# State-space sums in four row strips and four PSUM banks, VectorE's jobs in a new order, and the second attention's heads split as they are normed

## The chip, the cores and the metric

The kernel runs on one core of one Trainium2 chip. Its time is device time in microseconds (us). Before the change three runs took 2142.61, 2143.15 and 2150.36 us; their median, 2143.15 us, is the time before. All stages run one after another on the same core, and five engines work side by side: TensorE (PE in the profile, its weight loads PEld), VectorE (DVE), ScalarE (ACT), GpSimd (POOL) and SyncE (SP), which issues the DMAs.

## The reference, cut to what matters

The program is two layers of a hybrid block (attention, convolution, retention, MLP) and then one block of another kind, on 512 positions of width 1024, all in float32. The change lies in the last block:

```python
xn = rmsnorm(h, norm1_gain)
q, k, v, u, gates = split(xn @ w_in)
q = rope(rmsnorm(q, q_norm_gain)); k = rope(rmsnorm(k, k_norm_gain))
# 8 heads, each a difference of two softmaxes; o is 512 x 128 per head
o = diff_attention(q, k, v, lam)
attn_branch = rmsnorm(o, subln_gain) * (1 - lam_init) @ w_attn_proj
# s5: u (512 wide) -> complex states x_t = lb * x_{t-1} + B u_t, y = Re(C x) + D u
xr, xi = scan(lb, u @ B);  y = C_re @ xr - C_im @ xi + d * u
s = gelu(y) * sigmoid(gelu(y) @ w_glu + b_glu);  ssm_branch = s @ w_ssm_proj
h = h + (sigmoid(g_attn) * attn_branch + sigmoid(g_ssm) * ssm_branch) @ w_out
```

## The kernel before, in words

Nearly all of the time goes to dense products in a three-term form. Each float32 operand is split into a high and a low part (fp32r), and a product is hi*hi + lo*hi + hi*lo. A **piece** is twelve such matmuls of 128x128 weights by 512 columns (`accumulate`, L711 is its matmul). Four pieces use one weight unit of 1 MB. For each unit SP loads `raw`, ACT copies the high part (`w_hi`, L1356) and POOL subtracts to make the low part (`w_lo`, L518).

Each engine has a program of its own, written out in order. They meet only at semaphores. `fullN` says that PSUM bank N holds a result, `freeN` that it may be written again; `fill(b)` on PE waits for `freeN`. A tuple of numbers says behind which piece each side job stands: `p` counts the pieces of the last block's input products, and PE runs `hook(p)` behind piece p, while ACT and DVE walk through the same p and put their share at the same place in their own order. PE waits only where a semaphore is late.

The jobs of the stage that the change touches:

- **State sums.** For each of four blocks of 128 channels: `sums_in(blk)` on PE (L1010, behind pieces 8, 12, 16, 20) multiplies the inputs `uT` by `b_pow` into banks 4 (real) and 5 (imaginary). Each matmul has only 32 rows; the rows lie in one of four strips of the array, and two strips run at a time. After each of four rounds PE waits for `strip_done`. `states(blk, stage)` on DVE turns the sums by sine and cosine (stage 0, six instructions, L2341 to L2349), runs eight scans (stage 1, L2355) and turns back (stage 2, six instructions, L2360 to L2366). `sums_out(blk)` on PE (L1024, L1031, behind pieces 14, 18, 22, 26) waits for the states; `skip` on DVE (L2371) adds the input and frees bank 6.
- **Turn tables.** `turns(b)` on POOL (L643 to L648, six instructions) makes the sine and cosine of block b, between the `w_lo` units of this stage.
- **The kernel of the short response.** `short_response` (L995) behind piece 10.
- **Norm of q by columns.** `q_columns(n)` on PE (L1041, behind pieces 9 and 17) makes the mean squares of eight half heads, with 128 columns of `q_square` as weights and two moving columns, sixteen matmuls. DVE copies them out (`q_mean`, L2381) and so frees bank 7.
- **Rotation.** ACT moves a partner tile by four DMAs (`fetch_partner`, L1692; the third and later wait for the rotation two before), DVE rotates (`rotate`, L2398 to L2401, three instructions).
- **Norm of k.** `k_mean(j)` on PE (L1051) behind pieces 22, 24, 26, 28, 30, 36, 38 and 42; it fills bank 7, which the norm of the k before frees.

After the pieces comes the second attention: 32 steps (8 heads of 4 tiles), with 32 gate pieces laid between them by `GATE_STEPS`. PE makes scores (L822), transposes (L1116) and values (L1129). When a head is whole, ACT squares it (`o_square`, L1827), PE takes its mean (L822 too, `one(O_MEAN, ...)`), ACT and DVE take the root and norm the head. The gate pieces read `act_hi` and `act_lo`, and the normed heads are split into the same two tiles, so all eight splits stand at steps 32 to 37 (`heads_split`), behind the last gate pieces. The attention's projection starts after that.

## Time and profile before

| What | Value |
|---|---|
| median of three runs | 2143.15 us (2142.61 to 2150.36) |
| the profiled execution | 2144.72 us, its span 2142.9 us |
| PE busy | 2100.7 us, 98% of the span |
| DVE, ACT, POOL busy | 1061.5, 876.3, 925.4 us |
| pieces 9 to 30 with their jobs | 1296.7 to 1423.4 us from the span's start |
| second attention | 1511.6 to 1678.0 us |

All times are microseconds from the start of the span. A row of the timeline gives start, length, engine, line, operation, tiles and count; in square brackets the idle time before it and what ended that. Instructions of one engine overlap in the pipeline, so a matmul's own length is more than its share of time: the distance of starts tells the pace. PEclk is the clock that TensorE was granted, 1.00 being 2.4 GHz and 0.50 being 1.2 GHz.

### The profile page before, as it was taken

What the parts mean: (1) busy time and instruction counts of PE and PEld (TensorE: products, weight loads), DVE (VectorE), ACT (ScalarE), POOL (GpSimd) and SP (SyncE); (2) the same over time, 40 slices, a digit from 0 to 9 for tenths busy, and PEclk for the clock granted to TensorE, in tenths of its full rate; (3) what the DMA queues carried; (4) which work ended last, traced back from release to release, by engine and by line L of the source; (5) the groups of instructions that cost most, each with busy time, mean ns of one, the idle gap of its engine ahead of it and who ended that gap; (6) DMA issues with size and microseconds to landing.
All of it is one profiled execution on the core that took longest, in us unless ns stands there. A gap on an engine that the chain in (4) does not pass through costs nothing.

```text
span 2142.9 us, 27507 instructions
## 1 busy us (share of the span) xinstructions
PE 2100.7 (98%) x10200; PEld 1676.2 (78%) x10200; DVE 1061.5 (50%) x1725; ACT 876.3 (41%) x1219; POOL 925.4 (43%) x306
## 2 busy tenths in 40 slices
PE   8999999999999999999999999999999899999999
PEld 7875888888888776888888888877766787888887
DVE  5866242222247654422222258985588534554555
ACT  5345462223243445533222343164566534333332
POOL 5522444443455333545654456333312254444442
PEclk9999999999999999999999998899999999999999
DMA  5431213223224331233222242223111232322232
GB/s 182 150 117 71 77 63 98 97 98 98 99 69 149 125 93 46 79 99 98 94 100 87 92 148 85 66 84 108 60 60 60 95 100 81 97 88 90 97 98 78
DMA packets 120050, 202.29 MB, mean 94 GB/s; under 512 B 6544, under 2 KB 51856, under 8 KB 119696
## 3 DMA queue, kind: packets, MB, share of 16 engines
q1 hardware_dynamic: 112992, 189.12, 26.7%
q10 hardware_dynamic: 6960, 11.88, 1.9%
q8 instruction: 60, 0.98, 0.2%
q14 instruction: 38, 0.31, 0.0%
HBM read 189.44 MB, written 8.12 MB: 92 GB/s over the span
## 4 chain that ended last, share of the span: by engine, by line
PE 75%; issue 16%; POOL 3%; DVE 3%; ACT 1%; ACTq 1%; DMA 0%; POOLq 0%; DVEq 0%; SPq 0%
PE bank L711 63%; PE bank L813 5%; POOL w_lo L518 3%; PE bank L822 1%; PE bank L1010 1%; PE bank L765 1%; PE bank L840 1%; PE bank L880 1%; PE bank L774 1%; PE bank L868 0%; ACTq L1572 0%; DVE pr L2018 0%; PE bank L1041 0%; ACTq L1692 0%; PE bank L906 0%
## 5 line engine op out<-in xcount | busy, mean ns | idle before, releaser
L518 POOL TENSOR_TENSOR w_lo<-raw,w_hi 128x2048 fp32r<-128x2048 f32 (+1 forms) x167 | 741.9, 4442 | 1119.3 <-ACT w_hi L1356 1119.3
L711 PE MATMUL bank<-act_hi,w_hi 128*128 128x512 f32 x1488 | 595.6, 400 | 5.9 <-DVE hid L2561 2.5
L711 PE MATMUL bank<-act_hi,w_lo 128*128 128x512 f32 x1488 | 584.7, 393 | 0.0
L711 PE MATMUL bank<-act_lo,w_hi 128*128 128x512 f32 x1488 | 584.1, 393 | 0.0
L1356 ACT ACTIVATE w_hi<-raw 128x2048 fp32r<-128x2048 f32 (+1 forms) x170 | 314.2, 1848 | 591.2 <-PE bank L711 545.8
L711 PEld LDWEIGHTS bank<-act_hi,w_hi 128*128 128x128 f32 x1488 | 282.5, 190 | 78.0 <-issue 11.8
L711 PEld LDWEIGHTS bank<-act_hi,w_lo 128*128 128x128 f32 x1488 | 281.9, 189 | 60.7
L711 PEld LDWEIGHTS bank<-act_lo,w_hi 128*128 128x128 f32 x1488 | 282.5, 190 | 58.2 <-issue 1.4
L711 PE MATMUL bank<-h_hi,w_hi 128*128 128x512 f32 x704 | 277.7, 394 | 0.3 <-DVE x L2526 0.3
L711 PE MATMUL bank<-h_lo,w_hi 128*128 128x512 f32 x704 | 277.4, 394 | 0.0
L711 PE MATMUL bank<-h_hi,w_lo 128*128 128x512 f32 x704 | 277.4, 394 | 0.0
L2263 DVE TENSOR_TENSOR f<-f,bank 128x512 f32<-128x512 f32 x128 | 88.1, 688 | 238.7 <-PE bank L711 238.7
L2249 DVE SCALAR_TENSOR_TENSOR hid<-bank,rrow 128x512 f32<-128x512 f32 x64 | 43.7, 691 | 250.3 <-PE bank L711 245.3
L711 PEld LDWEIGHTS bank<-h_hi,w_hi 128*128 128x128 f32 x704 | 131.7, 187 | 33.4 <-DVE h_lo L2080 0.7
L711 PEld LDWEIGHTS bank<-h_hi,w_lo 128*128 128x128 f32 x704 | 131.7, 187 | 32.7
L711 PEld LDWEIGHTS bank<-h_lo,w_hi 128*128 128x128 f32 x704 | 131.7, 187 | 32.1
L2556 DVE TENSOR_TENSOR bank<-bank,rrow 128x512 f32<-128x512 f32 x44 | 30.7, 699 | 142.9 <-PE bank L711 140.4
L813 PE MATMUL bank<-act_hi,w_hi 128*128 128x512 f32 x192 | 76.3, 398 | 5.7 <-DVE act_lo L1940 5.2
L534 POOL TENSOR_TENSOR sums<-sums,squares 128x512 f32<-128x512 f32 x50 | 64.6, 1292 | 37.4 <-ACT squares L1374 35.1
L1993 DVE SCALAR_TENSOR_TENSOR bank<-ypad,lcol,bank 128x512 f32<-128x512 f32 x116 | 76.6, 755 | 0.0
L813 PE MATMUL bank<-act_hi,w_lo 128*128 128x512 f32 x192 | 74.8, 390 | 0.0
L813 PE MATMUL bank<-act_lo,w_hi 128*128 128x512 f32 x192 | 74.8, 389 | 0.0
(362 smaller groups left out, 2638.5 us busy)
## 6 DMA issues: line engine op xcount, KB each, us to landing
raw<-in_w_up SPq DMA_DIRECT2D x32, 1024.0 KB, 5.4
raw<-in_w_down SPq DMA_DIRECT2D x32, 1024.0 KB, 5.0
raw<-in_w_in SPq DMA_DIRECT2D x26, 1024.0 KB, 5.1
raw<-in_w_up SPq DMA_DIRECT2D x44, 512.0 KB, 4.6
raw<-in_w_in SPq DMA_DIRECT2D x28, 768.0 KB, 4.5
raw<-in_w_out SPq DMA_DIRECT2D x12, 1024.0 KB, 5.0
raw<-in_w_down SPq DMA_DIRECT2D x22, 512.0 KB, 4.2
raw<-in_w_attn_proj SPq DMA_DIRECT2D x4, 1024.0 KB, 5.1
```

Of the source, the lines that this page charges most:

```text
L518: pool.tensor_tensor(m.w_lo[slot][:, 0:n], m.raw[slot][:, 0:n], m.w_hi[slot][:, 0:n].bitcast(F32), ALU.subtract).then_inc(s["split_ready"], 1)
L534: ins = pool.tensor_tensor(m.sums[:], m.sums[:], m.squares[n % 4][:], ALU.add)
L711: mm = pe.matmul(o, ll if i == 2 else lh, rl if i == 1 else rh, start=first and n == 0, stop=last and n == len(steps) - 1)
L765: mm = pe.matmul(bank[b][:, t:t + 1], x[:, t * P:(t + 1) * P], m.per_d, start=(part == 0), stop=(part == 1))
L774: mm = pe.matmul(bank[b][:, t * P:(t + 1) * P], column[:, t:t + 1].to_broadcast([P, P]), m.ident, start=True, stop=True)
L813: mm = pe.matmul(bank[b][:], (wl if i == 2 else wh)[:, k % KU, cols], (m.act_lo if i == 1 else m.act_hi)[:, k, :], start=(k == 0 and i == ...
L822: pe.matmul(bank[b][:] if o is None else o, lhsT, rhs, start=True, stop=True).then_inc(s[f"full{b}"], 1)
L1356: act.activation(m.w_hi[slot][:, 0:n], m.raw[slot][:, 0:n], ACT.Copy).then_inc(s["w_hi"], 1)
L1993: ins = dve.scalar_tensor_tensor(to, y, w, sums, ALU.mult, ALU.add)
L2249: dve.scalar_tensor_tensor(m.hid[:, b, :], bank[b][:], 0.0, m.rrow[:], ALU.max, ALU.mult).then_inc(s[f"free{b}"], 1)
L2263: dve.tensor_tensor(sums, sums, bank[4 + b][:], ALU.add).then_inc(s[f"free{4 + b}"], 1)
L2556: dve.tensor_tensor(bank[b][:], bank[b][:], m.rrow[:], ALU.mult).then_inc(s["up_scaled"], 1)
```

## The change

What it does, part by part:

1. `sums_in` writes each row strip's sums to a bank of its own (4, 5, 6, 7; real part in columns 0 to 127, imaginary in 128 to 255). The four strips alternate matmul by matmul, and the waits for `strip_done` are gone. `states` reads all four banks as one tile of PSUM, and frees all four behind its fifth instruction. So `sums_in` now also needs banks 6 and 7.
2. `states` stages 0 and 1 stand one piece earlier, behind pieces 8 and 9, and so ahead of the rotations. The rotations are spread one per piece.
3. `q_columns` becomes two steps: `q_rows` (behind 10 and 18; four matmuls of 512 columns, each into 32 rows of bank 7), a copy by ACT, and four matmuls of 8 columns behind 11 and 19. In `jobs` on ACT the copy stands behind that piece's `fetch_partner`.
4. `short_response` moves from behind piece 10 to behind piece 6.
5. The turn tables get a tile per block. Block 0's is made during the layer before, blocks 1, 2 and 3 follow two units earlier than they did, behind the stage's first, second and third `w_lo`. They no longer wait for the states.
6. The normed heads are split into tiles of their own (`a_hi` over `k2`, `a_lo` over `q2`), each two steps behind its mean, so seven of the eight stand inside the attention. The mean stands a step later. Head 7's mean stands behind the first piece of the projection. The gate pieces stand in steps 0 to 27, 29, 31, 33 and 34.

The diff, cut to its core:

```diff
-        m.bank = [ctx.enter_context(nc.psum_tensor(f"bank{i}", [P, T], F32)) for i in range(8)]
+        m.bank = [ctx.enter_context(nc.psum_tensor(f"bank{i}", [P, T], F32)) for i in range(4)]
+        m.quad = ctx.enter_context(nc.psum_tensor("bank4", [P, 4, T], F32))
+        m.bank += [m.quad[:, i, :] for i in range(4)]
...
+    m.a_hi = ar("a_hi", [P, KD, T], 16, F32R)
+    m.a_lo = ar("a_lo", [P, KD, T], 0, F32R)
...
-    m.both = put("both", [P, T], at=x_at + 2048 * 5)
-    m.sin_n, m.cos_n = ([put(f"{name}{i}", [P, T], at=x_at + 2048 * (6 + k) if i == 0 else arena + 1024 * (36 + 2 * k)) for i in range(2)]
-                        for k, name in enumerate(("sin_n", "cos_n")))
+    m.both = ar("both", [P, T], 14)
+    m.sin_n, m.cos_n = ([ar(f"{name}{i}", [P, T], at + 2 * k) for i, at in enumerate((36, 28, 24))] +
+                        [put(f"{name}3", [P, T], at=x_at + 2048 * (5 + k))] for k, name in enumerate(("sin_n", "cos_n")))
...
+    def turns(b):
+
+        shape = [P, 4, TURN_A, TURN_B]
+        wide = lambda x: x[:].rearrange("p (s a b) -> p s a b", s=4, a=TURN_A)
+        sin, cos, both = wide(m.sin_n[b]), wide(m.cos_n[b]), wide(m.both)
...
+        if b == 3:
+            pool.wait_ge(s["x_parked"], 16)
...
-            for _ in range(U_MLP - 4 - 4 - 15):
+            lo()
+            for _ in turns(0):
+                lo()
+            for _ in range(U_MLP - 4 - 4 - 15 - 3):
...
-    pool.wait_ge(s["trig_ready"], 2)
+    whole(turns(1))
     lo()
-    turns(0)
+    whole(turns(2))
     lo()
-    turns(1)
-    lo()
-    turns(2)
-    lo()
-    turns(3)
-    lo()
-    lo()
+    whole(turns(3))
+    for _ in range(4):
...
-        fill(4)
-        fill(5)
+        for b in QUAD:
+            fill(b)
         if blk == 0:
             pe.wait_ge(s["u_ready"], 4)
             pe.wait_ge(s["param_dve"], N_PARAM_B)
-        for r in range(4):
+        for part in range(2):
             for j in range(SUB):
-                for part in range(2):
-                    q = (r + part) % 4
-                    mm = pe.matmul(bank[4 + part][:, q * P:(q + 1) * P], m.b_pow[strips[q], SUB - 1 - j, part, blk, :],
+                for q, b in enumerate(QUAD):
+                    mm = pe.matmul(bank[b][:, part * P:(part + 1) * P], m.b_pow[strips[q], SUB - 1 - j, part, blk, :],
                                    m.uT[strips[q], blk, j * N_SUB:(j + 1) * N_SUB], start=(j == 0), stop=(j == SUB - 1))
-                    if j == SUB - 1:
-                        mm.then_inc(s["strip_done" if r < 3 else f"full{4 + part}"], 1)
-            if r < 3:
-                pe.wait_ge(s["strip_done"], c.up("strip_done", 2))
+                    if part == 1 and j == SUB - 1:
+                        mm.then_inc(s[f"full{b}"], 1)
...
+    def q_rows(n):
 
         pe.wait_ge(s["q_squared"], c.up("q_squared", 4))
         fill(7)
         for j in range(4):
-            for t in range(NT):
-                mm = pe.matmul(bank[7][:, 0:8 * NT].rearrange("p (c j t) -> p c j t", c=2, t=NT)[:, :, j, t], m.q_square[j][:, t * P:(t + 1) * P],
-                               m.blk64.rearrange("p (c d) -> p c d", c=2)[:, :, 0], start=True, stop=True)
+            mm = pe.matmul(bank[7][strips[j], :], m.blk64.rearrange("p (c d) -> p c d", d=4)[:, :, 0], m.q_square[j][:], start=True, stop=True)
+        mm.then_inc(s["full7"], 1)
+
+    def q_columns(n):
+
+        fill(7)
+        for t in range(NT):
+            mm = pe.matmul(bank[7][:, 0:8 * NT].rearrange("p (c j t) -> p c j t", c=2, t=NT)[:, :, :, t], m.q_rows[:, t * P:(t + 1) * P],
+                           m.ident.rearrange("p (j c d) -> p c j d", j=4, c=2)[:, :, :, 0], start=True, stop=True)
...
+    def o_mean(h):
+
+        pe.wait_ge(s["o_squared"], c.up("o_squared"))
+        one(O_MEAN[h], m.avg128, m.o_square[:])
...
-    feature_major(4, ready=parts_ready)
-    feature_major(4)
+    between.append(lambda: o_mean(N_HEADS - 1))
+    feature_major(4, ah=m.a_hi, al=m.a_lo, ready=parts_ready)
+    feature_major(4, ah=m.a_hi, al=m.a_lo)
...
-TURN_BANKS, O_MEAN = (6, 3), 2
-ATT_STEPS = N_HEADS * NT + 6
-
-GATE_STEPS = [*range(27), 28, 29, 30, 32, 33]
+TURN_BANKS, O_MEAN = (6, 3), (2,) * (N_HEADS - 1) + (5,)
+ATT_STEPS = N_HEADS * NT + 9
+
+GATE_STEPS = [*range(28), 29, 31, 33, 34]
...
-def heads_split(i):
-
-    return {32: [0], 33: [1], 34: [2, 3], 35: [4, 5], 36: [6], 37: [7]}.get(i, [])
+def head_at(i, lag):
+
+    return (i - lag) // NT if i >= lag and (i - lag) % NT == NT - 1 and (i - lag) // NT < N_HEADS else None
...
-COLUMNS_AT, COLUMN_ROOT_AT = (9, 17), 18
+QUAD = (4, 5, 6, 7)
+ROWS_AT, COLUMNS_AT, COLUMN_ROOT_AT = (10, 18), (11, 19), 20
 K_AT = (22, 24, 26, 28, 30, 36, 38, 42)
-PARTNER_AT = (6, 7, 10, 10, 14, 15, 18, 18, 21, 22, 24, 26, 29, 34, 36, 40)
-ROTATE_AT = (8, 8, 12, 12, 16, 16, 20, 20)
+PARTNER_AT = (6, 7, 10, 11, 14, 15, 18, 19, 21, 23, 24, 26, 29, 34, 36, 40)
+ROTATE_AT = (8, 9, 12, 13, 16, 17, 20, 21)
...
-SHORT_AT = 10
+SHORT_AT = 6
...
-STATES_AT = ((9, 10, 11), (13, 14, 15), (17, 18, 19), (21, 22, 23))
+STATES_AT = ((8, 9, 11), (12, 13, 15), (16, 17, 19), (20, 21, 23))
...
         for j in jobs_at(p, PARTNER_AT):
             fetch_partner(j)
+        for n in jobs_at(p, ROWS_AT):
+            evac(7, m.q_rows[:])
         for n in jobs_at(p, COLUMNS_AT):
             use(7)
...
+        if meant(i) is not None:
+            inverse_root(O_MEAN[meant(i)], m.o_root[:], m.o_square[:])
+        if halved(i) is not None:
+            h = halved(i)
             act.wait_ge(s["o_normed"], h + 1)
-            copy_hi(m.act_hi[:, h, :], m.q2[:, h, :])
+            copy_hi(m.a_hi[:, h, :], m.q2[:, h, :])
...
         if stage == 0:
             dve.wait_ge(s["turned"], blk + 1)
-            full(4)
-            full(5)
-            dve.tensor_tensor(w0, bank[4][:], cos, ALU.mult).then_inc(s["dve_step"], 1)
-            dve.tensor_tensor(w2, bank[4][:], sin, ALU.mult).then_inc(s["free4"], 1)
+            for b in QUAD:
+                full(b)
+            re, im = (m.quad[:, :, part * P:(part + 1) * P] for part in range(2))
+            by_strip = lambda x: x.rearrange("p (q n) -> p q n", q=4)
+            dve.tensor_tensor(by_strip(w0), re, by_strip(cos), ALU.mult).then_inc(s["dve_step"], 1)
             c.up("dve_step")
-            link(dve.tensor_tensor(w1, bank[5][:], sin, ALU.mult))
+            dve.tensor_tensor(by_strip(w2), re, by_strip(sin), ALU.mult)
+            link(dve.tensor_tensor(by_strip(w1), im, by_strip(sin), ALU.mult))
             link(dve.tensor_tensor(w0, w0, w1, ALU.add))
-            dve.tensor_tensor(w1, bank[5][:], cos, ALU.mult).then_inc(s["free5"], 1)
-            freed(4)
-            freed(5)
+            link(dve.tensor_tensor(by_strip(w1), im, by_strip(cos), ALU.mult))
+            for b in QUAD:
+                dve.sem_inc(s[f"free{b}"], 1)
```

`meant(i)`, `normed(i)` and `halved(i)` are `head_at` with lags 6, 7 and 8.

The rows of each engine's order, at two places. On **DVE**, at the copy of the first column means (`q_mean`), before; `w` are the sums as they are turned, `bank` is PSUM:

```order
L2341 TENSOR_TENSOR w_116<-bank,cos_n_124 128x512
L2342 TENSOR_TENSOR w_118<-bank,sin_n_122 128x512
L2344 TENSOR_TENSOR w_117<-bank,sin_n_122 128x512
L2345 TENSOR_TENSOR w_116<-w_116,w_117 128x512
L2346 TENSOR_TENSOR w_117<-bank,cos_n_124 128x512
L2349 TENSOR_TENSOR w_117<-w_117,w_118 128x512
L2381 SCALAR_TENSOR_TENSOR q_mean<-small,bank 128x32
L2355 SCALAR_TENSOR_TENSOR w_116<-par,w_116 128x128
```

And in the changed kernel, at the same copy:

```order
L2400 TENSOR_TENSOR state_121<-w_118,cos_n_128 128x4x127
L2401 TENSOR_TENSOR w_120<-w_119,sin_n_124 128x4x127
L2402 TENSOR_TENSOR state_121<-state_121,w_120 128x4x127
L2403 TENSOR_TENSOR state_122<-w_118,sin_n_124 128x4x127
L2405 TENSOR_TENSOR w_120<-w_119,cos_n_128 128x4x127
L2406 TENSOR_TENSOR state_122<-state_122,w_120 128x4x127
L2421 SCALAR_TENSOR_TENSOR q_mean<-small,bank 128x32
L2381 TENSOR_TENSOR w_118<-bank,cos_n_129 128x512
```

The copy stood behind stage 0 of block 0 and ahead of its scans; now it stands behind all three stages of block 0 and both rotations between them, and the next instruction is block 1's stage 0.

On **PE**, at the end of the attention, before (`att` transposes, `pt` and `rope` values, `act_hi,w_hi` a gate piece above and the projection below):

```order
L711 MATMUL bank<-act_hi,w_lo_56 128x512
L1116 MATMUL bank<-cmat,att_147 128x128 x4
L1129 MATMUL bank<-pt_0_151,v_141 128x128 x3
L1129 MATMUL bank<-rope,v_141 128x128 x4
L822 MATMUL bank<-o_square,cmat 128x512
L711 MATMUL bank<-act_hi,w_hi_55 128x512
```

And in the changed kernel:

```order
L1134 MATMUL bank<-cmat,att_154 128x128 x4
L1145 MATMUL bank<-pt_0_158,v_148 128x128 x3
L718 MATMUL bank<-act_hi,w_hi_54 128x512
...
L718 MATMUL bank<-act_hi,w_lo_56 128x512
L1145 MATMUL bank<-rope,v_148 128x128 x4
L718 MATMUL bank<-a_hi,w_hi_55 128x512
...
L718 MATMUL bank<-a_hi,w_lo_57 128x512
L829 MATMUL bank<-o_square,cmat 128x512
```

A gate piece now stands between the last transposes and the last values, and the last head's mean behind the projection's first piece.

## Rows read from the trace of the kernel before

**Rows 1.** Page, busy time of each engine
```profile
PE 2100.7 (98%) x10200; PEld 1676.2 (78%) x10200; DVE 1061.5 (50%) x1725; ACT 876.3 (41%) x1219; POOL 925.4 (43%) x306
```

**Rows 2.** Stretches: length, busy PE, PEld, DVE, ACT, POOL, PEclk, DMA
```profile
1300.20:1306.90 6.70, 6.61 (x30) 5.22 (x28) 6.63 (x4) 0.66 (x1) 5.96 (x2) 0.50 0.03 4
...
1296.70:1423.40 126.70, 124.27 (x998) 101.04 (x997) 111.29 (x136) 33.88 (x46) 58.10 (x27) 0.89 0.24 71
```

**Rows 3.** Groups of PE from 1296.7 to 1423.4: busy, mean ns, idle before
```profile
L1010 PE MATMUL bank<-uT,b_pow 32*128 32x128 f32 x256 | 20.7, 305 | 1.1
...
L1041 PE MATMUL bank<-cmat,q_square 128*128 128x2 f32 x64 | 9.0, 275 | 0.0
```

**Rows 4.** Timeline of PE: two pieces' first matmuls, jobs, the fifth k mean
```profile
1289.84 0.39 PE L711 MATMUL bank<-act_hi,w_hi 128*128 128x512 f32 x1
...
1292.56 0.39 PE L711 MATMUL bank<-act_hi,w_hi 128*128 128x512 f32 x1
...
1296.73 5.93 PE L1010 MATMUL bank<-uT,b_pow 32*128 32x128 f32 x64
...
1316.89 2.09 PE L995 MATMUL bank<-ctab,braw 128*32 128x128 f32 x64
...
1324.58 4.92 PE L1010 MATMUL bank<-uT,b_pow 32*128 32x128 f32 x64
...
1423.38 1.10 PE L1051 MATMUL bank<-q_square,cmat 128*128 128x512 f32 x2 [1.32 <-DVE q_square L2073]
```

**Rows 5.** Timeline of the weight loads: the first round of the first sums
```profile
1296.73 0.97 PEld L1010 LDWEIGHTS bank<-uT,b_pow 32*128 32x128 f32 x16 [0.35 <-issue]
```

**Rows 6.** Timeline of DVE, first block's jobs, and one later rotation
```profile
1301.15 4.91 DVE L2401 TENSOR_TENSOR q<-q,partner 128x512 f32<-128x512 f32 x1
1306.10 1.43 DVE L2398 TENSOR_TENSOR partner<-partner,rope 128x512 f32<-128x512 f32 x1
...
1310.70 0.69 DVE L2341 TENSOR_TENSOR w<-bank,cos_n 128x512 f32<-128x512 f32 x1
...
1314.14 0.86 DVE L2349 TENSOR_TENSOR w<-w,w 128x512 f32<-128x512 f32 x1
...
1315.37 2.63 DVE L2355 TENSOR_TENSOR_SCAN w<-par,w 128x128 f32<-128x128 f32 x8
...
1321.28 0.69 DVE L2366 TENSOR_TENSOR state<-state,w 128x508 f32<-128x508 f32 x1
...
1379.17 0.69 DVE L2401 TENSOR_TENSOR q<-q,partner 128x512 f32<-128x512 f32 x1
```

**Rows 7.** Groups of DVE from 1296.7 to 1423.4, columns as in rows 3
```profile
L2401 DVE TENSOR_TENSOR q<-q,partner 128x512 f32<-128x512 f32 x8 | 16.5, 2058 | 0.3
```

**Rows 8.** Timeline of POOL: a low part, and one step of block 1's turn table
```profile
1300.94 4.58 POOL L518 TENSOR_TENSOR w_lo<-raw,w_hi 128x2048 fp32r<-128x2048 f32 x1 [0.97 <-ACT w_hi L1356]
...
1310.19 1.38 POOL L646 TENSOR_TENSOR cos_n<-turn_table 128x512 f32<-128x512 f32 x1
```

**Rows 9.** Timeline of ACT: partner DMAs, copies of the short response
```profile
1292.67 2.47 ACTq L1692 DMA_DIRECT2D partner<-q  x4
...
1319.13 2.44 ACT L1723 ACTIVATE taps<-bank 32x512 f32<-32x512 f32 x4 [18.27 <-PE bank L995]
```

**Rows 10.** Timeline of PE at the attention's end, idle time in brackets
```profile
1662.54 1.13 PE L822 MATMUL bank<-o_square,cmat 128*128 128x512 f32 x2 [1.74 <-ACT o_square L1827]
...
1672.75 1.16 PE L1129 MATMUL bank<-rope,v 128*128 128x128 f32 x8 [1.44 <-ACT rope L1816]
1674.59 1.12 PE L822 MATMUL bank<-o_square,cmat 128*128 128x512 f32 x2 [0.69 <-ACT o_square L1827]
1678.02 0.50 PE L711 MATMUL bank<-act_hi,w_hi 128*128 128x512 f32 x1 [2.30 <-DVE act_lo L2080]
```

**Rows 11.** Stretches of the attention's end, columns as in rows 2
```profile
1640.90:1670.30 29.40, 25.58 (x124) 18.34 (x125) 22.93 (x55) 17.47 (x40) 4.58 (x1) 1.00 0.11 37
...
1679.10:1682.40 3.30, 3.30 (x9) 2.59 (x8) 2.77 (x5) 0.42 (x1) 0.00 (x0) 0.50 0.70 271
```

84 lines of the change are left out of this document (47 added, 37 removed).

## The prediction, made before the changed kernel ran

> **What bounds the kernel now.** I read the busy times of the engines first: PE is busy for 2100.7 of 2142.9 us [rows 1]. So there is little idle time to take away, and a gain must come from PE's own work or from its clock. I then read stretches in turn, looking for PEclk below 1.00. Over pieces 9 to 30 (1296.7 to 1423.4) the mean granted clock is 0.89, and it is 0.50 in four stretches of at least 6.7 us, of which the first is shown [rows 2]; the others lie at 1310.5, 1354.9 and 1375.4. The timeline gives the pace of a piece: twelve matmuls from 1289.84 to 1292.56, 2.72 us [rows 4]. DVE is busy for 111.3 of the 126.7 us [rows 2], so it is nearly full in the stage in which PE is to become faster. The groups of DVE and the timelines of DVE, POOL and ACT show why [rows 6 to 9]. Last I read the attention's end, where PE has idle gaps [rows 10].
>
> **State sums.** They take 20.7 us busy and 1.1 us idle, 21.8 in four calls [rows 3]; an undisturbed call is 4.92 [rows 4]. A call is four rounds. The weight loads of a round (two strips) take 0.97 us for 16 records [rows 5], eight steps of some 0.11 us; a round lasts 4.92/4 = 1.23 us, so 0.26 of it is the wait at its end. With four strips abreast the 32 matmuls need 16 steps, 1.8 us, and one tail of 0.3: 2.1 us. The nearest row for four abreast is the short response, four strips of columns and also 64 records: 2.09 us [rows 4]. The other bound is that only two row strips run abreast, 32 steps and one tail, 3.9 us. I take 2.1, since the row with four abreast is nearer. Gain on PE: 21.8 - 8.4 = 13.4 us.
> The Trainium skill, "TensorE: Matmul & The Clock Gate", section "Measured speedup vs the span model", gives four row strips 3.07 times the rate of one, not four times. By it a call would be about 7.1/3.07 + 0.3 = 2.6 us (an estimate) and the four would gain 11.4 instead of 13.4 us on PE; no row here shows four row strips.
>
> **Column means.** Now 9.0 us for two calls [rows 3], 64 records. Afterwards a call is four matmuls of 8 columns, 8 records at the old 0.14 each or 1.1 us, and four of 512 columns side by side, two passes of 0.43 each (as a mean over 128x512 has, 1.1 us with its tail [rows 10]), 1.1 us. Two calls make 4.4, gain 4.6 us. If those four ran one after another: 3.5 us a call more than I take.
>
> **Clock.** Four stretches of 6.7 us at half speed lose 3.35 each, 13.4 us. Of it 2.1 us lie in the sums (21.8 less four times 4.92) and about 1.6 in the columns, and are counted above. If no stretch comes again, 9.7 us more. PE alone would then be 28 us faster up to the fifth k mean, and 29 with the 1.3 us it waited there [rows 4].
>
> **But DVE.** Its queue decides how much of the 29 us arrives. Its jobs between the first sums and the fifth k mean are the same in number: 111.3 us busy [rows 2]. They are that long because an instruction that reads twice from SBUF stands still while POOL works: 4.91 us beside a `w_lo` [rows 6, 8], 1.43 beside a turn table, 0.69 alone [rows 6]; one that reads PSUM keeps its 0.69 beside POOL (1310.70 beside POOL's 1310.19 [rows 6, 8]). The eight last steps of the rotations of q alone are 16.5 us instead of 8 x 0.69 = 5.5 [rows 7]; over all groups of DVE in this stage the excess over the shortest of each kind is 34 us. The six `w_lo` remain. Of the four turn tables, only block 3's now falls into the time behind the first sums. The turn tables' share in DVE's stretch I put at 9 us, and 4 of these remain: 106 us busy. DVE's idle time was 126.7 - 111.3 = 15.4 us; now it must still wait for each `sums_in` (2 us for block 1, 1 for the others) and for some of ACT's roots: 4.5 us. It starts at 1300.8 (the sums' end: 1296.6 + 2.1 short response, moved ahead, + 2.1), not at 1299.7. So it reaches the fifth k mean at 1300.8 + 106 + 4.5 = 1411 less the last norm's 2.2 us behind the mean: about 1409. **PE's gain there is about 15 us, not 29.**
>
> Where PE waits for it: the first place is behind pieces 11 and 12. `sums_in(1)` needs bank 7, which the copy of the column means frees. That copy stood behind stage 0; now block 0's three stages and two rotations stand ahead of it. DVE from 1300.8: stage 0 4.3 us (from 1310.70 to 1315.0 [rows 6]), rotation 2.1 (three of 0.69), scans 2.6, rotation 2.1, stage 2 3.9 and the copy 0.2: 15.3, and held up by the `w_lo` for about 4.5 and the turn table for 4.5: 1325. PE is there at 1300.8 + 4 x 2.72 + 2.2 = 1313.9. It waits 11 us. Some of it comes earlier, since ACT copies `q_rows` only behind its third `fetch_partner` (2.5 us [rows 9]), which waits for the first rotation: about 1316 for `q_columns(0)`, where PE stands at 1310. `sums_in(2)` needs bank 6 from `skip(0)`, behind block 1's rotations: DVE 1339, PE 1342, no wait. `sums_in(3)` needs both banks: within 2 us, up to 6 if a `w_lo` falls on stage 2. The rest of the 14 us, 1 to 3 us, is at the k means.
> PE's idle time may bring the low clock back. The attention's end shows it: 4.4 us of gaps in 8 us, then 0.50 for 3.3 us [rows 10, 11]. Beside DVE's lateness it costs little: piece 12 and block 1's sums.
> The Trainium skill says the same against this change ("TensorE: Matmul & The Clock Gate", section "HAM oscillation — how this bites in real kernels"): PE that idles between bursts is throttled again and again. By it the three waits would each cost up to 3.4 us if DVE were not late anyway; that is 7 to 10 us of the 14 us that PE loses to DVE, and nothing on top.
>
> **The other parts.** The short response only moves: 2.09 us, PE waits for nothing there; ACT's four copies (2.44 us [rows 9]) now stand ahead of a partner's DMAs and of a `w_hi`, 3 us later, with a unit's 10.9 us to spare. The tables of block 0 go to POOL beside the MLP, where it idles: nothing. Block 1's stands beside DVE's powers of b, 1 to 2 us later; they end at 1297, needed at 1298.7: nothing. Pieces 31 to the attention, 88 us: nothing, within 1.5 either way.
>
> **The attention's end.** From the last gate piece to the projection (1670.3 to 1678.0) PE idles 1.44 + 0.69 + 2.30 = 4.4 us [rows 10]. The gate piece at step 34 now covers the first, the mean behind the projection's first piece the second, and with seven heads split already the third goes. The 3.3 us at 0.50 cost 1.65 [rows 11]. Within the loop it idles 3.8 us from 1640.9 on (29.4 - 25.6 [rows 11]), mostly before steps that had no gate piece in front (1.74 of it in one place [rows 10]). Three steps instead of two now go without, one of them with no scores; I leave 2 us. Sum: 4.4 + 1.7 + 1.8 = 7.9, 8 us. What is late next is head 7's split. Behind the last gate piece come its values (0.9), the projection's first piece (2.7), the mean (1.1), then eight steps on ACT and DVE of about 0.7 us each: 10.4 us. The projection's second unit starts 0.9 + 4 x 2.72 + 1.1 = 12.9 us behind it. If that cover went, each us of lateness would count in full.
>
> **Sum.** 15 + 8 = 23 us off the profiled execution's 2144.7: 2121.7; it is 1.6 above the median, so 2120 to 2121. I say 2121.
>
> **Rivals.**
> 1. *PE-bound after all*: DVE's holds fall between its instructions, and the waits vanish: 29 + 9 = 38 us, 2105. For it: without any hold DVE's jobs are 111.3 - 34 = 77 us, and PE's own time for this stage is 126.7 - 29 = 98. Against it: six `w_lo` of 4.6 us stand beside them, and almost every one met a twofold SBUF reader. For 29 us most of the holds must go. Chance 0.13.
> 2. *DVE's queue costs more*: `sums_in(2)` and `(3)` each wait as `(1)` does, by one more hold of 4.3 us each and the low clock behind it, 9 us less, and the attention gives 6: 15 + 6 - 9 = 12 us, 2131. For it: every hold seen lasted 4 to 5 us. Chance 0.2.
> 3. *Slower*: lock step. PE stands idle while DVE works through a block, and DVE while PE does. Place: `fill(6)` and `fill(7)` of the three later sums. Price: PE's 98 us and DVE's 106 us of this stage add as far as they don't stand side by side; before, the stage took 126.7. It decides at 126.7 + 8 (the attention's gain) + 11 (0.5%) = 146 us, which is where only 98 + 106 - 146 = 58 us stand side by side. That time is 2155. Against it: in the sums above 85 us or more do. Chance 0.03.
> 4. *Strips not abreast*: 3.9 us a call, 7 us more on PE; DVE is the later one, so 3 us of it arrive: 2124, inside the forecast. A chance of 0.1 within it.
>
> **How the numbers follow.** Forecast 2114 to 2127, chance 0.64; rival 1 0.13 (2101 to 2114), rival 2 0.2 (2127 to 2138), rival 3 0.03. A change under 0.5% (10.7 us) can't be told from none. Rival 2 holds 0.06 of "same": faster 0.91, same 0.06, slower 0.03. The range for 8 in 10 takes half of rivals 1 and 2: 2109 to 2132.
>
> **What would show it.** Records of `sums_in` four at a time and a call at 2.1 us; no PEclk of 0.50 behind the sums; PE idle before `q_columns(0)` and `sums_in(1)`, together 10 to 13 us, released by ACT and DVE; the fifth k mean at 1405 to 1412; PE from the last gate piece to the projection without a gap. It is wrong if `sums_in(1)` waits under 5 us, or the time from the fifth k mean to the attention changes by over 2 us.

## The result, and the profile after

Six runs of the changed kernel took 2122.73 to 2131.27 us, median 2130.3; six of the kernel before, on the same chip, 2142.61 to 2152.23 us, median 2147.07. The ratio is 0.9918 with a 95% interval of 0.9898 to 0.9937: 17.6 us faster, between 13.5 and 21.9. The forecast was 2121, 22 us off the median of 2143.15. The median of 2130.3 lies outside its 2114 to 2127 and inside the wider range, 2109 to 2132. But the kernel before ran at 2147.07 here: by the ratio, 2143.15 becomes 2125.6, which lies in both.

The profiled execution took 2130.64 us, its span 2128.8 us, 14.1 less than before. The stretches that answer to those of before follow. Columns are length, busy PE, PEld, DVE, ACT, POOL, PEclk and DMA. For the kernel before: from the 7th to the 40th piece of the last block's products (the starts of `p` = 6 and 39; between them lie the short response, the state sums and the k means of either kernel), and from there to the 16th piece of the attention's projection:

```profile
1288.50:1450.80 162.30, 158.92 (x1138) 126.92 (x1136) 140.41 (x160) 57.81 (x76) 75.41 (x33) 0.92 0.27 82
1450.80:1720.60 269.80, 259.31 (x1205) 192.91 (x1205) 183.71 (x350) 151.52 (x283) 78.51 (x17) 0.99 0.22 74
```

The changed kernel: the same two stretches, then the part of the first from the first sums to the fifth k mean (which was 126.70 [rows 2]), and the first layer's first pieces:

```profile
1293.20:1446.60 153.40, 137.94 (x1107) 107.76 (x1105) 128.37 (x163) 58.66 (x77) 57.34 (x21) 0.97 0.30 86
1446.60:1706.50 259.90, 256.33 (x1205) 191.58 (x1204) 182.65 (x350) 151.86 (x283) 78.80 (x17) 0.99 0.23 77
1303.60:1418.90 115.30, 101.09 (x902) 80.23 (x901) 97.04 (x136) 33.34 (x46) 37.59 (x13) 0.96 0.26 74
...
12.20:39.90 27.70, 22.11 (x84) 17.79 (x85) 12.55 (x13) 17.74 (x27) 21.63 (x11) 0.88 0.29 93
```

So 8.9 us were gained in the sums' stage and 9.9 around the attention. The 7th piece starts 4.7 us later than before (1293.2 against 1288.5): 5.4 were lost in the first 45 us of the program, which no edit touches (last section), and 0.7 came back on the way. Apart from it the change gave this pair of executions 19 us.

PE's jobs in the stage are what the change says: L1017 are the state sums, L1045 the row means, L1052 the column means, L1029 the output of a block. Timeline of PE, changed kernel:

```profile
1303.58 2.07 PE L1017 MATMUL bank<-uT,b_pow 32*128 32x128 f32 x64
1311.24 1.09 PE L1045 MATMUL bank<-q_square,cmat 128*32 128x512 f32 x8
1321.78 1.88 PE L1052 MATMUL bank<-cmat,q_rows 128*128 128x8 f32 x8 [6.50 <-ACT q_rows L1394]
1330.23 3.53 PE L1017 MATMUL bank<-uT,b_pow 32*128 32x128 f32 x64 [2.02 <-DVE q_mean L2421]
1349.29 2.07 PE L1017 MATMUL bank<-uT,b_pow 32*128 32x128 f32 x64
1359.15 2.50 PE L1029 MATMUL bank<-uT,taps 128*128 128x128 f32 x20 [2.13 <-DVEq L2388]
1371.97 2.07 PE L1017 MATMUL bank<-uT,b_pow 32*128 32x128 f32 x64 [1.00 <-DVE q_mean L2421]
```

An undisturbed call takes 2.07 us instead of 4.92 [rows 4]. The second call takes 3.53, at the low clock. PE now stands idle for 115.3 - 101.1 = 14.2 us in the stage; before, its only wait there was 1.32 us [rows 4].

DVE in the first block, and ACT where PE waited 6.50 us:

```profile
1309.75 4.27 DVE L2389 TENSOR_TENSOR w<-w,w 128x512 f32<-128x512 f32 x1 [0.43 <-DVE w L2386]
1314.06 1.43 DVE L2438 TENSOR_TENSOR partner<-partner,rope 128x512 f32<-128x512 f32 x1
...
1318.65 5.20 DVE L2395 TENSOR_TENSOR_SCAN w<-par,w 128x128 f32<-128x128 f32 x8
...
1329.90 0.19 DVE L2421 SCALAR_TENSOR_TENSOR q_mean<-small,bank 128x32 f32<-128x32 f32 x1
```
```profile
1318.64 2.44 ACTq L1727 DMA_DIRECT2D partner<-q  x4
1321.13 0.60 ACT L1394 ACTIVATE q_rows<-bank 128x512 f32<-128x512 f32 x1 [12.33 <-issue]
```

A hold is the stretching of a DVE instruction beside one of POOL's. A low part's hold falls on stage 0 (4.27 us instead of 0.69), a turn table's on the rotation and the scans (5.20 instead of 2.63 [rows 6]). The rotation ends at 1318.6, only then do the partner's DMAs go out, and only behind them the copy for which PE waits. The waits of DVE on the others in the stage (us in total, times, longest):

```profile
DVE w L2381 <- PE bank L1017: 10.7, 4, 3.9
DVE q_square L2111 <- ACT q_square L1401: 2.7, 1, 2.7
```

PE waits for DVE's copy, and DVE then waits for PE's sums: 3.9 us for block 1.

The attention's end, changed kernel:

```profile
1662.75 1.05 PE L1145 MATMUL bank<-rope,v 128*128 128x128 f32 x8
1663.55 0.48 PE L718 MATMUL bank<-a_hi,w_hi 128*128 128x512 f32 x1
...
1666.44 1.02 PE L829 MATMUL bank<-o_square,cmat 128*128 128x512 f32 x2
```

No row has a wait in brackets: the gaps of 1.44, 0.69 and 2.30 us [rows 10] are gone.

### The profile page after: what moved, and what is told of

It is laid out like the page before. It is cut to its first block, busy times and chain, and to the rows that moved or that the text cites. A ratio compares the mean times of both kernels' runs of the same rounds, so it can differ in the third digit from the quotient of the medians.

```text
span 2128.8 us, 27453 instructions
## 1 busy us (share of the span) xinstructions
PE 2081.8 (98%) x10168; PEld 1660.9 (78%) x10168; DVE 1050.8 (49%) x1725; ACT 877.0 (41%) x1221; POOL 922.1 (43%) x306
## 4 chain that ended last, share of the span: by engine, by line
PE 75%; issue 15%; DVE 5%; POOL 3%; ACT 0%; DMA 0%; ACTq 0%; DVEq 0%; POOLq 0%
PE bank L718 63%; PE bank L820 5%; POOL w_lo L523 3%; PE bank L829 1%; PE bank L796 1%; PE bank L772 1%; PE bank L847 1%; PE bank L887 1%; PE bank L875 1%; PE bank L1017 0%; PE bank L781 0%; DVE w L2395 0%; DVE pr L2056 0%; PE bank L913 0%; DMA tmul<-in_tmul 0%
## 5 line engine op out<-in xcount | busy, mean ns | idle before, releaser
L718 PE MATMUL bank<-act_hi,w_hi 128*128 128x512 f32 x1424 | 567.7, 399 | 3.6 <-DVE hid L2604 2.5
L718 PE MATMUL bank<-act_hi,w_lo 128*128 128x512 f32 x1424 | 556.8, 391 | 0.0
L718 PE MATMUL bank<-act_lo,w_hi 128*128 128x512 f32 x1424 | 556.4, 391 | 0.0
L718 PEld LDWEIGHTS bank<-act_hi,w_hi 128*128 128x128 f32 x1424 | 268.7, 189 | 73.0 <-issue 13.0
L718 PEld LDWEIGHTS bank<-act_hi,w_lo 128*128 128x128 f32 x1424 | 268.2, 188 | 57.7
L718 PEld LDWEIGHTS bank<-act_lo,w_hi 128*128 128x128 f32 x1424 | 268.6, 189 | 55.0 <-issue 1.4
L820 PE MATMUL bank<-act_hi,w_hi 128*128 128x512 f32 x192 | 77.6, 404 | 5.7 <-DVE act_lo L1978 5.5
L820 PE MATMUL bank<-act_lo,w_hi 128*128 128x512 f32 x192 | 75.8, 395 | 0.0
L820 PE MATMUL bank<-act_hi,w_lo 128*128 128x512 f32 x192 | 75.7, 395 | 0.0
```

The costliest lines, as they stand in the source:

```text
L718: mm = pe.matmul(o, ll if i == 2 else lh, rl if i == 1 else rh, start=first and n == 0, stop=last and n == len(steps) - 1)
L820: mm = pe.matmul(bank[b][:], (wl if i == 2 else wh)[:, k % KU, cols], (m.act_lo if i == 1 else m.act_hi)[:, k, :], start=(k == 0 and i == ...
```

## The experiments

Each kernel gave one trace and 4 to 12 runs. Its ratio is taken against runs of the kernel before on the same chip (medians of 2145.9 to 2151.0 us, of which the table has one); the two stretches are those shown above.

| Kernel | median us | ratio to before [95%] | 7th to 40th piece | 40th to projection |
|---|---|---|---|---|
| before | 2147.07 | | 162.3 | 269.8 |
| changed | 2130.3 | 0.9918 [0.9898, 0.9937] | 153.4 | 259.9 |
| tail_only | 2131.11 | 0.9932 [0.9909, 0.9956] | 158.1 | 259.9 |
| stage_only | 2136.73 | 0.9958 [0.9943, 0.9973] | 152.1 | 269.7 |
| no_tables | 2117.83 | 0.9876 [0.9852, 0.9900] | 147.5 | 259.9 |
| columns_first | 2129.5 | 0.9921 [0.9898, 0.9943] | 154.2 | 259.9 |
| both_first | 2127.99 | 0.9901 [0.9870, 0.9932] | 155.1 | 260.1 |
| short_at_10 | 2125.16 | 0.9890 [0.9857, 0.9923] | 150.2 | 261.5 |
| two_abreast | 2129.26 | 0.9919 [0.9891, 0.9947] | 155.8 | 259.9 |
| psum_first | 2126.02 | 0.9893 [0.9859, 0.9927] | 151.2 | 260.0 |
| filler | 2127.99 | 0.9915 [0.9894, 0.9935] | 153.6 | 260.0 |
| combo_scp | 2125.82 | 0.9907 [0.9891, 0.9924] | 149.2 | 259.9 |
| combo_all | 2120.85 | 0.9884 [0.9865, 0.9902] | 149.5 | 259.9 |
| combo_fill | 2120.15 | 0.9891 [0.9874, 0.9909] | 147.5 | 259.9 |

The intervals of the ratios are 6 to 14 us wide and overlap; the verdicts below go by the stretches of the traces, of which each is one execution. How far the first stretch moves by itself shows in two pairs of executions with the same instructions there: before and tail_only, 162.3 and 158.1; changed and stage_only, 153.4 and 152.1. In the second pair nearly all of the difference is block 1's sums, 3.53 us at the low clock in the one and 2.07 in the other. So kernels whose block 1 sums took 2.07 are better held against stage_only's 152.1, and a difference of 1 to 2 us between single traces proves little.

**tail_only.** The kernel before with part 6 alone (the heads' splits, their means and the gate steps).

> The kernel before with part 6 alone (heads split in tiles of their own two steps behind their means, gate pieces in steps 0 to 27, 29, 31, 33, 34). Theory A, the two halves of the change add: the trace of the changed kernel stands 4.2 us ahead of the one before at the start of the attention and 14.1 us ahead some 20 us behind its end, so 9.8 us belong to part 6; this kernel gains 9 to 10 us, a ratio near 0.9955, and its sums stage lasts 126.7 us as before. Theory B, part of those 9.8 us is inherited from the earlier stages (banks and buffers free sooner): it gains 5 us or less, a ratio above 0.9977.

The stretch around the attention is 259.9 us, 9.9 less, as in the changed kernel. That is theory A. By its times the kernel gains 14.6 us (9.4 to 19.5), which can't narrow it down. The sums' stage was to last as before, and took 4.2 us less. Columns as above; stage, then attention:

```profile
1287.90:1446.00 158.10, 151.56 (x1139) 120.86 (x1137) 139.06 (x160) 57.76 (x76) 75.08 (x33) 0.97 0.28 83
1446.00:1705.90 259.90, 254.52 (x1204) 190.19 (x1204) 182.63 (x350) 151.91 (x283) 78.79 (x17) 1.00 0.23 77
```

The mean clock in the stage is 0.97 against 0.92, with nothing changed in it: how often the low clock comes there differs from one execution to the next. PE's waits in it rose from 3.4 us (162.3 - 158.9) to 6.5 as it ran faster, 5.4 of them ended by DVE: it was the next bound already before the change. The attention ran without any low clock and took the same 259.9 us as the changed kernel did with PEclk 0.99.

**stage_only.** The changed kernel with part 6 undone.

> The changed kernel with part 6 undone. Theory A, the halves add: the stage from piece 8's job to the fifth k mean lasts 117.4 us as in the changed kernel against 126.7 before (9.3 less), PE idles some 14 us in it, and the attention's end has its gaps of 1.44, 0.69 and 2.30 us back; ratio near 0.9955. Theory B: more than 9.3 us or less than 5 us arrive, since the low clock is granted at other places once the end is different; ratio outside 0.993 to 0.998. Also read here: whether the start-up (first layer's first pieces) has the late table load and the low clock that the changed kernel's profiled run has; if that is a matter of chance, some of these traces are without it.

The stage is 152.1 us, the attention 269.7, with the gaps of 1.45, 0.69 and 2.29 us back. By its times it gains 9.0 us (5.8 to 12.2). In the stretches the halves give 9.9 and 10.2 us, and the whole 18.8. By the times they give 14.6 and 9.0, and the whole 17.6: they add, within what these can tell.

**no_tables.**

```diff
-    whole(turns(1))
...
-    whole(turns(2))
...
-    whole(turns(3))
...
-        sin, cos = m.sin_n[blk][:], m.cos_n[blk][:]
+        sin, cos = m.sin_n[0][:], m.cos_n[0][:]
```

> The changed kernel without the turn tables of blocks 1 to 3 (those blocks turn by block 0's table, so their values differ from the reference; every other instruction stays). Theory A, VectorE's queue from the first sums to the copy of the column means sets the stage: beside the tables its rotation took 1.43 + 1.53 + 1.63 instead of 3 x 0.69 and its scans 5.20 instead of 2.63, 5.1 us in all; with them gone the copy comes 5 us sooner, PE's waits of 6.50 and 2.02 us shrink together by 4 to 5 us, and the stage lasts 113 us or less. Theory B, PE or ScalarE sets it and VectorE's holds lie in idle time: the stage lasts 117 us as before, ratio to the changed kernel 1.000.

The stage is 5.9 us shorter, 147.5; no other kernel got lower. The scans take 2.63 us again, and the column copy comes 1317.33 - 1296.12 = 21.2 us behind the start of the first sums instead of 26.3. PE's two waits of 6.50 and 2.02 us became one of 3.95. The rows are of DVE's timeline:

```profile
1308.64 2.63 DVE L2392 TENSOR_TENSOR_SCAN w<-par,w 128x128 f32<-128x128 f32 x8
...
1317.33 0.19 DVE L2418 SCALAR_TENSOR_TENSOR q_mean<-small,bank 128x32 f32<-128x32 f32 x1
```

Theory A: the copy came 5.1 us sooner, as expected, and the stage followed. DVE's queue from the first sums to that copy is what binds. Block 1's sums ran at the full clock here, so against stage_only the gain is 4.6 us. The tables cannot be left out, and no kernel here has them at another place.

**columns_first.** In DVE's `jobs`:

```diff
-        for n in jobs_at(p, COLUMNS_AT):
+        for n in jobs_at(p + 1, COLUMNS_AT):
             q_columns(n)
```

> The changed kernel with VectorE's copy of the column means ahead of stage 2 of the states instead of behind it (for both column groups). Theory A, sums_in(1) waits for that copy and VectorE then waits for the sums: the copy comes 3.9 us sooner, PE's wait of 2.02 us before sums_in(1) goes, and VectorE's idle time before block 1 falls from 3.93 to some 2 us; the stage is 2 us shorter for block 1 and up to 1 us for block 3 (wait of 1.00 us). Theory B, all that counts is ScalarE's late copy of the row means (6.50 us): nothing changes, the stage lasts 117.4 us.

`sums_in(1)` starts 25.3 us behind the first sums instead of 26.65, a gain of 1.3, and then the stage is 0.8 us longer than the changed kernel's, 2.1 longer than stage_only's. Two waits of PE took it back:

```profile
1351.75 2.50 PE L1029 MATMUL bank<-uT,taps 128*128 128x128 f32 x20 [2.37 <-DVEq L2388]
1374.41 0.88 PE L1029 MATMUL bank<-uT,taps 128*128 128x128 f32 x5 [3.19 <-DVEq L2388]
```

L2388 is DVE's release of the four banks, behind the fifth instruction of stage 0. `sums_out` needs bank 6, which since this change `sums_in` fills too. In the trace of the changed kernel the wait was 2.13 us. There a low part on POOL stretched the addition ahead of the release, from 0.69 to 4.52 us:

```profile
1353.60 4.52 DVE L2385 TENSOR_TENSOR w<-w,w 128x512 f32<-128x512 f32 x1
1358.16 0.69 DVE L2386 TENSOR_TENSOR w<-bank,cos_n 128x512 f32<-128x512 f32 x1
```

**both_first.** The same, and in ACT's `jobs`:

```diff
+        for n in jobs_at(p, ROWS_AT):
+            evac(7, m.q_rows[:])
         for j in jobs_at(p, PARTNER_AT):
             fetch_partner(j)
-        for n in jobs_at(p, ROWS_AT):
-            evac(7, m.q_rows[:])
```

> The changed kernel with both orders turned: ScalarE copies the row means ahead of the partner's DMAs, VectorE copies the column means ahead of stage 2 of the states. Theory A, bank 7 binds PE behind pieces 11 and 12 and VectorE's copy is the last link: PE passes q_columns(0) without its wait of 6.5 us but then waits that much longer before sums_in(1), which starts right behind the second rotation, some 23.5 us behind sums_in(0) (26.65 in the changed kernel, 25.3 with the column copy alone first). Stage about 2 to 3 us shorter than the changed kernel's. Theory B, ScalarE's copy alone was the cause: the 6.5 us go and do not come back, sums_in(1) starts 20 us or less behind sums_in(0), and the stage is 6 us shorter.

```profile
1312.65 0.95 PE L1052 MATMUL bank<-cmat,q_rows 128*128 128x8 f32 x8
1323.86 3.80 PE L1017 MATMUL bank<-uT,b_pow 32*128 32x128 f32 x64 [7.42 <-DVE q_mean L2421]
```

The wait before `q_columns(0)` is gone and stands before `sums_in(1)`: 7.42 us, 22.75 us behind the first sums. For block 1 theory A is right, and 3.9 us are won there. The stage is nevertheless 1.7 us longer. Waits for bank 6 took 6.0 us in all (the longest 3.2), and the sums ran at the low clock.

**short_at_10.**

```diff
-SHORT_AT = 6
+SHORT_AT = 10
```

> The changed kernel with the short response behind piece 10 again. Theory A: the first sums start 2.0 us sooner and with them VectorE's whole queue, while the short response fills 2.0 us of PE's wait of 6.5 us behind piece 11; the time from piece 7's start to the fifth k mean is 2 us shorter. Theory B: PE's own work sets the end of the stage, and it only moves: no change beyond 0.5 us; its rival within B is that PE's shorter idle time lets the low clock of 6.83 us behind it go, another 2 to 3 us.

The stage is 3.2 us shorter. PE's wait behind piece 11 fell from 6.50 to 4.84 us, since the short response now lies in it. From piece 7 to the fifth k mean it is 122.0 us instead of 125.7. Theory A accounts for 2.0 of the 3.7. `sums_in(1)` ran at the full clock here (2.07 instead of 3.53 us), which accounts for most of the rest. That isn't the edit's doing: in stage_only, where the short response stands as in the changed kernel, these sums took 2.07 too. Against stage_only the stage is 1.9 us shorter, which is theory A alone.

**two_abreast.**

```diff
-        for part in range(2):
-            for j in range(SUB):
-                for q, b in enumerate(QUAD):
+        for pair in ((0, 1), (2, 3)):
+            for part in range(2):
+                for j in range(SUB):
+                    for q in pair:
```

> The changed kernel with the four strips taken in two pairs, one pair behind the other, the banks and all waits as they are. If the pair's steps cost what the first round's loads did (0.97 us for 16), a call lasts 3.9 us instead of 2.07. Theory A, VectorE waits at each call for its sums (2.75, 3.93, 1.57 and 2.48 us in the changed kernel), so the 1.8 us of each call arrive nearly whole: the stage is 5 to 7 us longer. Theory B, as the prediction had it: VectorE's queue is late by itself, and of the 7 us about 3 arrive.

A call takes 3.51 us against 2.07. Four calls are 5.8 us more work on PE, and the stage grew by 2.4 us against the changed kernel and 3.7 against stage_only. Nearer to theory B, half of it arrives. Of the 2.85 us that a call became shorter, half came with the missing waits for `strip_done` (4.92 to 3.51) and half with four strips instead of two (3.51 to 2.07).

**psum_first.**

```diff
-            link(dve.tensor_tensor(by_strip(w1), im, by_strip(sin), ALU.mult))
-            link(dve.tensor_tensor(w0, w0, w1, ALU.add))
-            link(dve.tensor_tensor(by_strip(w1), im, by_strip(cos), ALU.mult))
+            dve.tensor_tensor(by_strip(w1), im, by_strip(sin), ALU.mult)
+            link(dve.tensor_tensor(by_strip(w3), im, by_strip(cos), ALU.mult))
             for b in QUAD:
                 dve.sem_inc(s[f"free{b}"], 1)
-            link(dve.tensor_tensor(w1, w1, w2, ALU.subtract))
+            link(dve.tensor_tensor(w0, w0, w1, ALU.add))
+            link(dve.tensor_tensor(w1, w3, w2, ALU.subtract))
```

> The changed kernel with stage 0 of the states in another order: all four products that read PSUM first (a fourth tile takes the last one), then the release of the four banks, then the two that read SBUF twice. Theory A, PE's waits of 2.13 us before sums_out(1) (and of 2.37 and 3.19 us in the run with the column copy first) are for bank 6, held while a low part on GpSimd stretched the SBUF addition between the products: no such wait is left, and PE is 2 us ahead there; as VectorE's queue is no shorter, of these 2 us between 0 and 2 reach the fifth k mean. Theory B: the wait stays, since it is for something else than the release of the banks.

```profile
1345.86 2.07 PE L1017 MATMUL bank<-uT,b_pow 32*128 32x128 f32 x64
1353.43 2.39 PE L1029 MATMUL bank<-uT,taps 128*128 128x128 f32 x20
```
```profile
1350.06 0.68 DVE L2385 TENSOR_TENSOR w<-bank,cos_n 128x512 f32<-128x512 f32 x1
1351.16 3.39 DVE L2388 TENSOR_TENSOR w<-w,w 128x512 f32<-128x512 f32 x1 [0.42 <-DVE w L2385]
```

The hold is still there (3.39 us at 1351.16), now behind the release, and PE has no wait at 1353.43. The stage is 2.2 us shorter than the changed kernel's and 0.9 shorter than stage_only's, in which block 1's sums ran at the full clock as they do here. Theory A, by the wait; of its 2 us about 1 arrives. The new order has a price too: the hold now takes 5.15 us of block 0's stage 0, and the column copy comes 27.0 us behind the first sums instead of 26.3.

**filler.** In PE's `hook`, ahead of its jobs:

```diff
+        if p == 11:
+            emptied(4)
+            for _ in range(24):
+                pe.matmul(bank[4][:], m.act_hi[:, 0, 0:P], m.act_hi[:, 1, :], start=True, stop=True)
```

> The changed kernel with 24 matmuls of 512 columns more on PE behind piece 11, into bank 4, which nobody reads before the next sums overwrite it: 24 x 0.227 = 5.4 us of work in a wait of 6.5 us. Theory A, PE's low clock of 6.8 and 3.4 us in the changed kernel (10.2 us in most of the other runs) follows the wait, and what it costs is the part of VectorE's path that runs through PE: q_columns(0) at half speed (1.88 against 0.95 us) and sums_in(1) (3.53 against 2.07 us). Without the idle time there is no PEclk of 0.50 between 1310 and 1340, and from the first sums to the fifth k mean it is 1.5 to 2.5 us shorter than 115.3. Theory B, the low clock comes from the sums or from piece 12 and not from the wait: it stays. Theory C, the low clock lies wholly in time in which PE waits anyway: it goes, and the 115.3 us stay.

PE's wait is filled and `q_columns(0)` takes 1.06 us instead of 1.88: no low clock there. It came at the next wait instead:

```profile
1319.79 1.06 PE L1052 MATMUL bank<-cmat,q_rows 128*128 128x8 f32 x8 [1.11 <-ACT q_rows L1398]
1328.26 3.80 PE L1017 MATMUL bank<-uT,b_pow 32*128 32x128 f32 x64 [4.53 <-DVE q_mean L2425]
```

The sums take 3.80 us, and the stage is 153.6 us, as in the changed kernel (to the fifth k mean 115.5 us, against 115.3). The half of theory A that says that the low clock follows the wait is right, its gain did not come, since a wait remained.

**combo_scp and combo_all.** The edits of short_at_10, columns_first and psum_first together; combo_all has the edit of both_first too.

> Three orders together on the changed kernel: the short response behind piece 10, VectorE's column copy ahead of stage 2, and stage 0's four PSUM products ahead of the release and of the SBUF additions. Alone they gave from piece 7 to piece 40 (153.4 us in the changed kernel) 150.2, 154.1 and 151.2. Theory A, what the column copy won for block 1 (1.3 us) was lost again at bank 6 (waits of 2.37 and 3.19 us), which the new stage 0 takes away, so all three add: 153.4 - 3.1 - 1.3 - 2.2 = 147 us. Theory B, each of them only moves the wait, and the next one in line (ScalarE's copy of the rows, column copy of the second group) takes over: 150 us, no better than the best alone.

> As the three orders together, and ScalarE's copy of the row means ahead of the partner's DMAs too. Theory A, VectorE's queue is what binds block 1's sums, so this copy adds nothing to the other three: within 1 us of them from piece 7 to piece 40, with PE's wait before q_columns(0) turned into one before sums_in(1). Theory B, PE's idle time then lies in one piece right before the sums, the low clock falls on them (3.80 instead of 2.07 us in the run with the two copies alone), and it is 1.5 us or more slower than without it.

149.2 and 149.5 us, by which theory B of the first (150) and theory A of the second would hold. PE's rows speak against both. Two of combo_scp, then one of combo_all:

```profile
1303.12 2.07 PE L1017 MATMUL bank<-uT,b_pow 32*128 32x128 f32 x64 [1.92 <-DVEq L2364]
1326.59 2.07 PE L1017 MATMUL bank<-uT,b_pow 32*128 32x128 f32 x64
```
```profile
1318.62 3.79 PE L1017 MATMUL bank<-uT,b_pow 32*128 32x128 f32 x64 [5.46 <-DVE q_mean L2421]
```

The first sums of combo_scp waited 1.92 us for DVE's powers of b (`b_pow`). No edit touches these; but the short response, now behind piece 10, no longer covers it when they come late. DVE had waited 3.42 us for the load of `lam` in that execution, and 2.00 in combo_all's, where PE had no such wait. Without it combo_scp's stage is 147.3 us, which is theory A's 147: the three orders add. Counted from the start of the first sums to piece 40, it is 139.0 us in combo_scp, 141.3 in combo_all, 143.0 in the changed kernel and 141.7 in stage_only. So with ACT's copy first the stage is 2.3 us slower, and block 1's sums took 3.79 us at the low clock: that is theory B of the second. Each rests on one trace. The times point the other way (2125.82 and 2120.85 us), with intervals that overlap.

In both, PE still waits for bank 6 behind piece 22, here in combo_all:

```profile
1368.08 3.81 PE L1029 MATMUL bank<-uT,taps 128*128 128x128 f32 x20 [2.26 <-DVEq L2387]
```

Here the hold fell on stage 2, ahead of block 3's stage 0, and no order within stage 0 helps. combo_all has the lowest median without extra work, 2120.85 us and a ratio of 0.9884 against the changed kernel's 0.9918. That is 7 us, of which the stage shows 4; the intervals overlap, and the rest is not explained.

**combo_fill.** combo_all with filler's matmuls in the wait before `sums_in(1)`; against filler's edit:

```diff
-        if p == 11:
+        if p == 12:
             emptied(4)
-            for _ in range(24):
+            for _ in range(20):
```

> The four orders together and 20 matmuls of 512 columns more on PE (20 x 0.227 = 4.5 us) in the wait of 5.46 us that PE has right before sums_in(1), into bank 4, which the sums overwrite. Theory A, with the wait filled there is no low clock on the sums of block 1, which take 2.07 us instead of 3.79, VectorE gets them 1.7 us sooner, and from piece 7 to piece 40 it is 1.5 to 2.5 us shorter than the 149.6 without the extra matmuls. Theory B, as with the 24 matmuls before q_columns(0), the low clock only moves to another place (the wait of 2.3 us before sums_out(2), or the pieces behind the sums): 149 to 150 us.

PE's timeline, and the stretch from piece 7 to 1365.0:

```profile
1310.57 4.70 PE L1073 MATMUL bank<-act_hi 128*128 128x512 f32 x20
1317.02 2.07 PE L1017 MATMUL bank<-uT,b_pow 32*128 32x128 f32 x64 [1.75 <-DVE q_mean L2425]
```
```profile
1285.40:1365.00 79.60, 75.19 (x752) 61.85 (x752) 72.06 (x96) 22.61 (x32) 38.91 (x17) 1.00 0.32 94
```

PEclk is 1.00 in this stretch (3.4 us at 1.2 GHz follow at 1365.2, as they do in combo_all), and the sums take 2.07 us instead of 3.79; the stage is 147.5 us, 2.0 less, by work that computes nothing. From the first sums to piece 40 it is 139.2 us instead of 141.3. Theory A: 2 us is what the low clock costs there, though PE waits anyway. The times (0.9891 against 0.9884) can't tell the two apart.

## Why the prediction was right, and what it missed

**State sums and column means: right.** 2.1 us a call was predicted and 2.07 measured. The other bound, two strips abreast, is 3.51 us (3.9 was predicted). A pair of column mean jobs takes 1.09 + 0.95 = 2.04 us; 2.2 was predicted. By the Trainium skill, "TensorE: Matmul & The Clock Gate", section "Measured speedup vs the span model", a call would have been about 2.6 us (an estimate); the trace shows 2.07.

**Where PE waits for DVE: right in place and in size.** The column copy was put 26.3 us behind the start of the first sums (1325 less 1298.7), and stands at 1329.90 - 1303.58 = 26.3. ACT's copy of the rows was put at 17.3, and came at 17.55. The two waits come to 6.50 + 2.02 = 8.5 us; 11 were predicted, the rest lies in PE's slower piece and means between them. By its own words the prediction would be wrong if `sums_in(1)` waited under 5 us. It waited 2.02, since the wait had moved ahead to `q_columns(0)`; when both_first took the earlier one away, 7.42 us stood at `sums_in(1)`. That test was badly put, the mechanism stands. `sums_in(2)` didn't wait, `sums_in(3)` 1.00 us, the k means 2.4. Missed was `sums_out(1)`, 2.13 us for bank 6: the prediction gave `sums_in` the wait for bank 6, but not `sums_out` the wait for `sums_in`'s use of it. All waits together are 14.2 us and 14 were predicted. That the totals agree is in part luck, since 2.5 us too much at the first two places stand against the 2.13 that were missed.

**The step that failed: "Beside DVE's lateness it costs little".** The gain in the stage was put at 15 us, as if only waits stood against the 29. PE's work in the stage at the full clock is 126.7 - 29.0 = 97.7 less the 2.1 of the short response, 95.6 us. It was busy for 101.1, which is 5.5 more. The low clock behind the wait of 6.50 us, as a window of the changed kernel:

```profile
1320.40:1327.10 6.70, 5.32 (x17) 4.55 (x18) 6.60 (x12) 0.60 (x1) 1.51 (x2) 0.50 0.12 29
```

5.32 us of work at 1.2 GHz are 2.7 us lost; block 1's sums took 3.53 instead of 2.07, 1.5 more. These 4.2 us are most of the 5.5. The wait was long enough to bring the clock down and too short to hide all of it. So 29 - 14.2 - 5.5 = 9.3 us, and 8.9 in the longer windows. This is PE's own account. It doesn't say that the full clock would give all of it back, since PE would then wait longer for DVE: stage_only, with the full clock on block 1's sums, is 1.3 us shorter, and combo_fill 2.0 shorter than combo_all. In both_first, filler and combo_all a wait of over 4 us right before block 1's sums brought 1.2 GHz on them (3.80, 3.80 and 3.79 us); with the wait filled it was gone. The rule of the Trainium skill that the prediction weighed and put at "nothing on top" ("TensorE: Matmul & The Clock Gate", section "HAM oscillation — how this bites in real kernels") is that PE falls back to the low clock when it idles between bursts of matmuls. These traces agree with it.

**DVE's sum was nearly right only by two errors.** It was to be busy for 106 us and idle for 4.5. It was busy for 97.0 from its first sums to the fifth k mean, 9 less, and idle for 15.9, 11 more. The holds add up to 20 us here, where the trace before had 34 (over the shortest of each kind). The two errors belong together: of the six low parts of POOL two (at 1330.47 and 1371.32) ran while DVE waited for sums or read PSUM, and held nothing. Of the idle time 10.7 - 2.75 = 8.0 us are waits for the sums of blocks 1 to 3 (4 were predicted) and 2.7 for ACT's root. The lock step that the prediction feared as rival 3 is there, but small: PE waits for DVE's copy, the clock falls, the sums come late, DVE waits.

**Clock: half right.** The calls of the new sums and means ahead of which PE had not waited brought no stretch at 0.50. The changed kernel has two in the stage, one from within the wait of 6.50 us (1320.4) and one from 0.4 us into block 1's sums (1330.6), behind the wait of 2.02. The four stretches at 0.50 of the trace before were not a constant of that kernel, though: in tail_only the same stage had a mean clock of 0.97 and ran 4.2 us shorter. A part of the gain of 8.9 us in the pair of traces may therefore be chance; how large it is, is not shown. By their times stage_only gives 9.0 us (5.8 to 12.2).

**The attention's end: right, somewhat small.** 8 us predicted, and 9.7 to 9.9 measured in eleven of the twelve traces with part 6. In short_at_10 it is 8.3, where 3.4 us at 1.2 GHz fell right at the start of the stretch. PE's idle time fell from 269.8 - 259.3 = 10.5 to 3.6 us, 6.9 less; the rest is its busy time, with 1.65 for the low clock at the projection's start. Head 7's split was in time.

**The sum.** 8.9 + 9.9 = 18.8 instead of 23, where 5.5 us that PE was busy longer, most of it at the low clock, and 1.9 more from the attention are the largest terms. The result is 17.6. PE-bound (rival 1) is excluded by PE's 14.2 idle us. Rival 2 has about the time that was measured, but not its mechanism: `sums_in(2)` and `(3)` did not wait as `(1)` did.
